# Half of the recurrence's input loads issued from ScalarE's queue instead of SyncE's

## The chip, the cores and the metric

The kernel runs on one core of a Trainium2 chip. The metric is the time of one execution on the device in microseconds (us). In what follows SP is SyncE, which here does nothing but issue transfers and wait; PE is TensorE, DVE is VectorE, ACT is ScalarE and POOL is GpSimd.

## What is computed

One step of a decoder layer for 2048 prompt tokens and 64 sample tokens (8 sequences of 8). A combined projection feeds two head groups, a chunked spatial gating and an S5 state-space layer; their outputs are merged by one projection, and a mixture of experts follows. The change lies in the S5 layer, whose core is a recurrence over positions:

```python
bu_re = jnp.einsum('blgh,gph->blgp', u, br)      # 32 groups of 16 channels, 64 complex states each
_, _, h_re, h_im = lax.associative_scan(ssm_combine, (a_re, a_im, bu_re, bu_im), axis=1)
y = (jnp.einsum('blgp,ghp->blgh', h_re, c_re) - jnp.einsum('blgp,ghp->blgh', h_im, c_im) + d_skip * u)
y = jax.nn.gelu(y.reshape(Bn, L, D_B))
```

## The kernel before

The program is a row of blocks with a barrier between them: the front (projections, tables), `s5` (the recurrence, 576 to 792 us of the span), `mixout`, routing, the experts and the final rows. In each block every engine has a hand-written list of instructions, ordered against the others by semaphores only.

**Layout in s5.** The prompt is cut into 128 chunks of 16 positions (Q = 16). `uT` holds the layer's input with a position within the chunk and a channel on the partitions: partition block m (16 partitions, the 16 channels of a group) holds position 7 - m of the first eight positions in `uT[:, 0]`, and position 15 - m in `uT[:, 1]`. The free axis runs over the 32 groups and over CH = 136 columns, 8 for the sample sequences and 128 for the chunks. The input lies in HBM (`s_d`, `ss_d`), written by the block before. One part of `uT`, eight groups, is loaded by `load_u(i)`: for two halves (kt) and eight blocks (m) one transfer of 64 KB for the prompt (L1243) and one of 4 KB for the samples (L1244), so 32 issues for a part and four parts in all.

**Tables.** `tab` has four slots and holds for a pair of groups what the recurrence multiplies by (768 KB, L1249); slot p % 4 may be loaded again when TensorE has finished the outputs of pair p - 4. `toep` (eight transfers of 256 KB, L1258) holds the part of the result that stays within eight positions.

**Work of a batch** b of two pairs. TensorE's `additions(b)` (L1319) makes the chunk's contribution to the state, from `uT` and `tab`; VectorE's `batch(b)` (L1407 to L1427) turns and scans it into the states `h`; TensorE's `outputs(2b)` and `outputs(2b+1)` (L1335, L1337, L1342) make the result, ScalarE puts it through gelu (L1383), and SP stores it with 24 transfers (L1270, L1273). TensorE's order is additions 0 and 1, then for each b: outputs 2b, outputs 2b+1, additions b+2. `additions(2j)` waits for part j of `uT`.

**SP's order**: tables 0 and 1, the two initial states, `load_u(0)`, `toep`, tables 2 and 3; then for each batch b: `load_u(b + 1)` while b < 3, tables 2b+4 and 2b+5, the 24 stores of batch b, which wait for its gelus.

**ScalarE's order**: it waits for TensorE's transpose of the initial states (`h0_mm`), copies them into `h` (L1373), makes the upper parts of two pieces of `w_glu` (`hi(0)`, `hi(1)`, L1369), and then does the gelus, with one more `hi` per batch. VectorE makes the matching lower parts (`low(0)`, `low(1)`, L1394) before `batch(0)`, and one `low` before each later batch. GpSimd loads the weights' pieces (L1297), from the third on each waiting for a `low`.

Of the kernel before, what the change touches and what calls it, by code (L numbers as in the profile page):

```python
# [41 lines left out]
GC = 16  # L42
# [4 lines left out]
CH = NCH + NSEQ  # L47
# [106 lines left out]
def build(nc, a, o):  # L154
    ctx = ExitStack()
    with ctx:
# [42 lines left out]
        with ExitStack() as mid:  # L199
            S.wout_hi = sb(mid, "wout_hi", [P, KD, D], F32R)  # L200
            S.wout_lo = sb(mid, "wout_lo", [P, KD, D], F32R)
            S.wglu_hi = sb(mid, "wglu_hi", [P, 4, DA], F32R)
            S.wglu_lo = sb(mid, "wglu_lo", [P, 4, DA], F32R)
            S.w_l = sem("weights_lo")
            s5(nc, S, a, o)
            spent.close()
            mixout(nc, S, a)
# [981 lines left out]
def s5(nc, S, a, o):  # L1189
    with ExitStack() as st:  # L1190
        sb, sem = S.sb, S.sem
        NB = 4
        uT = sb(st, "uT", [P, 2, G, CH])
        tab = sb(st, "tab", [P, NB, TABW])
        toep = sb(st, "toep", [P, G, P])
        h = sb(st, "h", [P, PAIRS, 2, CH + 1])
# [14 lines left out]
        u_ld = [sem(f"uT_loaded{i}") for i in range(4)]  # L1211
# [10 lines left out]
        N = NSEQ  # L1222

        def part(t_glu, t_out, n):
            return t_glu[:, 2 * n:2 * n + 2, :] if n < 2 else t_out[:, n - 2, :]

        def raw_part(n):
            return raw[:, n % 2, :].rearrange("p (k n) -> p k n", k=2) if n < 2 else raw[:, n % 2, :]

        w_glu, w_out = (t[0].rearrange("(k p) n -> p k n", p=P) for t in (a.w_glu, a.w_out))  # L1230

        with nc.Block() as block:
            @block.sync
            def _(sp):
                s_rows = S.s_d.rearrange("(g h) s c -> s h g c", h=GC)
                ss_rows = S.ss_d.rearrange("(g h) t q -> t h g q", h=GC)

                def load_u(i):
                    gs = slice(8 * i, 8 * i + 8)
                    for kt in range(2):  # L1240
                        for m in range(8):
                            rows = slice(m * GC, (m + 1) * GC)
                            sp.dma_start(uT[rows, kt, gs, N:CH], s_rows[8 * kt + 7 - m, :, gs, :]).then_inc(u_ld[i], 16)  # L1243
                            sp.dma_start(uT[rows, kt, gs, 0:N], ss_rows[7 - m, :, gs, :]).then_inc(u_ld[i], 16)  # L1244

                def load_tab(p):
                    if p >= NB:
                        sp.wait_ge(y_mm, 2 * (p - NB) + 2)
                    sp.dma_start(tab[:, p % NB, :], S.tab_d[p]).then_inc(tab_ld[p % NB], 16)  # L1249

                for p in range(2):
                    load_tab(p)
                for i, t in enumerate((a.state_ssm_re, a.state_ssm_im)):
                    sp.dma_start(h0_in[:, i, :], t[0].rearrange("q (a g) p -> (q a) (g p)", g=2)).then_inc(h0_ld, 16)
                load_u(0)
                for m in range(8):
                    s = 7 - m
                    sp.dma_start(toep[m * GC:(m + 1) * GC, :, :], S.kpad_d[:, :, P - s * GC:2 * P - s * GC]).then_inc(toep_ld, 16)  # L1258
                for p in range(2, 4):
                    load_tab(p)  # L1260

                def store_y(b):
                    g0 = 4 * b
                    sp.wait_ge(y_ok, 4 * b + 4)
                    for half in range(2):
                        for m in range(8):
                            dst = S.y_d.rearrange("(g o) s c -> s o g c", o=GC)[8 * half + m, :, g0:g0 + 4, :]
                            rows = slice(m * GC, (m + 1) * GC)
                            lo = N if half == 0 else CH
                            sp.dma_start(dst, ys[rows, b % 2, :, lo:lo + NCH]).then_inc(y_out[b % 2], 16)  # L1270
                    for m in range(8):
                        dst = S.ys_d.rearrange("(g o) t q -> t o g q", o=GC)[m, :, g0:g0 + 4, :]
                        sp.dma_start(dst, ys[m * GC:(m + 1) * GC, b % 2, :, 0:N]).then_inc(y_out[b % 2], 16)  # L1273

                for b in range(NBATCH):
                    if b < 3:
                        load_u(b + 1)
                    for p in (2 * b + 4, 2 * b + 5):
                        if p < PAIRS:
                            load_tab(p)  # L1280
                    store_y(b)
                sp.wait_ge(f_ok, 4)
                for i, (p, q) in enumerate(((o.ssm_re_prompt, o.ssm_re_sample), (o.ssm_im_prompt, o.ssm_im_sample))):
                    sp.dma_start(p[0, 0].rearrange("(a g) p -> a (g p)", g=2), po[:, i, :]).then_inc(f_out, 16)
                    sp.dma_start(q[0].rearrange("q (a g) p -> (q a) (g p)", g=2), fo[:, i, :]).then_inc(f_out, 16)
                sp.wait_ge(f_out, 64)
                for n in range(2):
                    sp.wait_ge(y_out[n], 16 * 24 * (NBATCH // 2))
# [76 lines left out]
            @block.scalar  # L1365
            def _(act):
                def hi(n):
                    act.wait_ge(raw_ld[n % 2], 16 * (n // 2) + 16)
                    act.activation(part(S.wglu_hi, S.wout_hi, n), raw_part(n), ACT.Copy).then_inc(w_h, 1)  # L1369

                act.wait_ge(h0_mm, 1)
                for i in range(2):
                    act.activation(h[:, :, i, 0:N], pY[:, 3, i * P:(i + 1) * P].rearrange("p (q a) -> p a q", q=NSEQ),  # L1373
                                   ACT.Copy).then_inc(h0_ok, 1)
                hi(0)
                hi(1)
                for p in range(PAIRS):
                    b = p // 2
                    for g in range(2):
                        act.wait_ge(y_mm, 2 * p + 2)  # L1380
                        if b >= 2:
                            act.wait_ge(y_out[b % 2], 16 * 24 * (b // 2))
                        act.activation(ys[:, b % 2, 2 * (p % 2) + g, 0:CH + NCH], pY[:, (2 * p + g) % 4, 0:CH + NCH],  # L1383
                                       ACT.Gelu_apprx_tanh).then_inc(y_ok, 1)
                    if p % 2 and p // 2 + 2 < 10:
                        hi(p // 2 + 2)
# [1174 lines left out]
```

## Time and profile before

| | |
|---|---|
| median of three runs | 1841.05 us (1839.16 to 1841.66) |
| the profiled execution | 1843.49 us, span 1841.4 us |
| TensorE busy, whole span | 1320.4 us, 72% |
| VectorE, ScalarE, GpSimd busy | 1012.7, 564.0, 387.5 us |
| mean granted TensorE clock | 0.839 of full speed |
| from 576 to 793 us: TensorE, VectorE, ScalarE busy | 92.2, 61.5, 20.6 us of 217 |

Busy time doesn't count the issuing of transfers, so SP's load is read from the timeline of its queue: start, duration of the issue, and the transfer's name. In a timeline the bracket at the end is the idle time before the instruction and who ended it. The DMA share is the mean busy share of the core's 16 DMA engines; it can exceed 1 where transfers of one engine overlap.

### The profile page before, as it was taken

The page shows a single profiled execution, that of the slowest core. Times are in us where ns is not written, and L with a number is a line of the kernel's source. Part 1 is how long each engine was busy: PE and PEld are TensorE (multiplying, and loading weights), DVE is VectorE, ACT ScalarE, POOL GpSimd, SP SyncE. Part 2 cuts the span into 40 slices and gives each one's busy share as a digit, 9 for nine tenths or more (in the row PEclk, how much of TensorE's full clock was granted, in tenths as well). Part 3 has the DMA queues.
Part 4 walks back from the last instruction along what each step waited for, and adds up shares of the span by engine and source line. Part 5 has one row for each costly group of instructions (what it writes and reads, how often), then busy time and mean ns, then how long its engine had stood idle before and what let it go on. Part 6 is the DMA issues. An engine that isn't in the chain of part 4 may idle for free. (4 is left out here: it accounts for less than half of the span.)

```text
span 1841.4 us, 25617 instructions
## 1 busy us (share of the span) xinstructions
PE 1320.4 (72%) x6602; PEld 1068.6 (58%) x6603; DVE 1012.7 (55%) x2397; ACT 564.0 (31%) x874; POOL 387.5 (21%) x392
## 2 busy tenths in 40 slices
PE   1466587999993435518888988379999999999300
PEld 0256465778872334417777876258777877777200
DVE  2355424776742233316666755858645477576398
ACT  2343320111111000113323221037645467566121
POOL 0020000222210000010010000035633337455321
PEclk9577688999997566759989998569999999999755
DMA  5966454753425945275544711269977679996597
GB/s 167 286 190 181 109 152 104 245 182 123 161 79 132 160 113 166 76 218 153 162 134 154 227 69 57 67 222 361 382 273 246 220 259 381 327 332 249 209 340 277
DMA packets 289969, 365.69 MB, mean 199 GB/s; under 512 B 125969, under 2 KB 229713, under 8 KB 286818
## 3 DMA queue, kind: packets, MB, share of 16 engines
q1 hardware_dynamic: 264770, 278.20, 48.3%
q0 software_dynamic: 25120, 86.53, 13.8%
q8 instruction: 38, 0.62, 0.1%
q14 instruction: 41, 0.34, 0.1%
HBM read 256.62 MB, written 108.04 MB: 198 GB/s over the span
## 5 line engine op out<-in xcount | busy, mean ns | idle before, releaser
L2222 POOL TENSOR_TENSOR down_lo<-expert_raw,down_hi (+1 forms) x64 | 153.1, 2415 | 198.2 <-ACT down_hi L2316 198.2
L2366 DVE TENSOR_TENSOR up_lo<-expert_raw,up_hi (+1 forms) x128 | 161.7, 1322 | 19.8 <-ACT up_hi L2311 17.3
L247 PE MATMUL ps_up<-up_hi,xT_hi 128*128 x400 | 161.5, 404 | 6.3 <-DVE up_lo L2366 2.9
L248 PE MATMUL ps_up<-up_lo,xT_hi 128*128 x400 | 156.7, 392 | 0.0
L249 PE MATMUL ps_up<-up_hi,xT_lo 128*128 x400 | 156.4, 391 | 0.0
L1610 PE MATMUL ps_out<-wout_hi,catT 128*128 128x512 f32 (+1 forms) x272 | 111.1, 408 | 24.5 <-DVE h L1764 22.1
L2311 ACT ACTIVATE up_hi<-expert_raw (+1 forms) x128 | 125.1, 1057 | 1.7 <-issue 0.5
L1611 PE MATMUL ps_out<-wout_lo,catT 128*128 128x512 f32 (+1 forms) x272 | 109.2, 402 | 0.0
L1612 PE MATMUL ps_out<-wout_hi,catT 128*128 128x512 f32 (+1 forms) x272 | 109.0, 401 | 0.0
L793 PE MATMUL ps_a<-hT,win_s 128*128 128x384 f32 (+2 forms) x160 | 69.9, 437 | 30.4 <-DVE sT L1089 30.3
L247 PEld LDWEIGHTS ps_up<-up_hi,xT_hi 128*128 128x128 f32 x400 | 75.5, 189 | 26.4 <-issue 11.7
L1319 PE MATMUL ps_state<-uT,tab 128*64 128x136 f32 (+1 forms) x256 | 28.6, 395 | 79.7 <-DMA tab<-s_tables 44.0
L249 PEld LDWEIGHTS ps_up<-up_hi,xT_lo 128*128 128x128 f32 x400 | 75.5, 189 | 16.2
L248 PEld LDWEIGHTS ps_up<-up_lo,xT_hi 128*128 128x128 f32 x400 | 75.6, 189 | 14.2
L2360 DVE TENSOR_TENSOR xT_lo<-ps_xT,xT_hi 128x512 fp32r<-128x512 f32 x102 | 65.7, 686 | 22.6 <-ACT xT_hi L2304 22.2
L249 PE MATMUL ps_y<-down_hi,hidT_lo 128*128 x196 | 77.6, 396 | 0.0
L247 PE MATMUL ps_y<-down_hi,hidT_hi 128*128 x196 | 77.5, 396 | 0.0
L248 PE MATMUL ps_y<-down_lo,hidT_hi 128*128 x196 | 77.5, 396 | 0.0
L2304 ACT ACTIVATE xT_hi<-ps_xT 128x512 fp32r<-128x512 f32 x102 | 55.4, 598 | 69.3 <-PE ps_xT L2252 68.9
L1576 POOL DMA_DIRECT2D expert_rows<-blank x31 | 26.8, 984 | 232.7 <-DVE x L1767 228.8
L1610 PEld LDWEIGHTS ps_out<-wout_hi,catT 128*128 128x128 f32 (+1 forms) x272 | 52.3, 192 | 37.9 <-DVE h L1764 22.6
L1394 DVE TENSOR_TENSOR wout_lo<-weights_raw,wout_hi 128x1024 fp32r<-128x1024 f32 x8 | 9.8, 1226 | 116.8 <-ACT wout_hi L1369 116.8
(392 smaller groups left out, 3180.0 us busy)
## 6 DMA issues: line engine op xcount, KB each, us to landing
expert_raw<-in_w SPq DMA_DIRECT2D x96, 1024.0 KB, 7.8
expert_rows<-yo SPq DMA_DIRECT2D x49, 512.0 KB
x<-in_x_prompt SPq DMA_DIRECT2D x32, 512.0 KB, 5.2
stage<-in_w_ada SPq DMA_DIRECT2D x16, 1024.0 KB
expert_rows<-blank POOLq DMA_DIRECT2D x31, 512.0 KB, 5.6
tab<-s_tables SPq DMA_DIRECT2D x16, 768.0 KB, 4.6
h_turned<-hT SPq DMA_DIRECT2D x48, 192.0 KB, 2.1
hT<-h_turned SPq DMA_DIRECT2D x48, 192.0 KB, 2.9
```

The lines of the kernel that those rows point to most:

```text
L247: pe.matmul(out, left(0, k), right(0, k), start=k == 0, stop=False)
L248: pe.matmul(out, left(0, k), right(1, k), start=False, stop=False)
L249: last = pe.matmul(out, left(1, k), right(0, k), start=False, stop=k == n - 1)
L793: pe.matmul(out[:, j, 0:w], hi[:, k, cols], hT[:, 0, k, 0:w], start=k == 0, stop=False)
L1610: pe.matmul(out, cat[:, 0, k, ts], S.wout_hi[:, k, cols], start=k == 0, stop=False)
L1611: pe.matmul(out, cat[:, 0, k, ts], S.wout_lo[:, k, cols], start=False, stop=False)
L1612: last = pe.matmul(out, cat[:, 1, k, ts], S.wout_hi[:, k, cols], start=False, stop=k == KD - 1)
L2222: pool.tensor_tensor(down_piece(down_lo, run, m), raw_piece(run, 2, m, 1), down_piece(down_hi, run, m).bitcast(F32), ALU.subtract).then_in ...
L2304: act.activation(xT_hi[:, par, 4 * h:4 * h + 4, :], pX[:, h, :].rearrange("p (k t) -> p k t", k=4), ACT.Copy).then_inc(x_a, 1)
L2311: act.activation(up_piece(up_hi, run, m), raw_piece(run, m // 2, m % 2, KD // 2), ACT.Copy).then_inc(up_h, 1)
L2360: dve.tensor_tensor(xT_lo[:, par, ks, :], pX[:, h, :].rearrange("p (k t) -> p k t", k=4), xT_hi[:, par, ks, :].bitcast(F32), ALU.subtract) ...
L2366: dve.tensor_tensor(up_piece(up_lo, run, m), raw_piece(run, m // 2, m % 2, KD // 2), up_piece(up_hi, run, m).bitcast(F32), ALU.subtract).t ...
```

## The change

The second half of every part (kt = 1, positions 8 to 15 of a chunk) is issued by ScalarE. SP keeps the first half. ScalarE issues its 4 x 16 transfers at the head of the block, ahead of its first wait; SP's order is otherwise the same. The semaphores and the counts that TensorE waits for (32 transfers a part) stay.

```diff
+        s_rows = S.s_d.rearrange("(g h) s c -> s h g c", h=GC)
+        ss_rows = S.ss_d.rearrange("(g h) t q -> t h g q", h=GC)
+
+        def load_half(eng, i, kt):
+            gs = slice(8 * i, 8 * i + 8)
+            for m in range(8):
+                rows = slice(m * GC, (m + 1) * GC)
+                eng.dma_start(uT[rows, kt, gs, N:CH], s_rows[8 * kt + 7 - m, :, gs, :]).then_inc(u_ld[i], 16)
+                eng.dma_start(uT[rows, kt, gs, 0:N], ss_rows[7 - m, :, gs, :]).then_inc(u_ld[i], 16)
+
         with nc.Block() as block:
             @block.sync
             def _(sp):
-                s_rows = S.s_d.rearrange("(g h) s c -> s h g c", h=GC)
-                ss_rows = S.ss_d.rearrange("(g h) t q -> t h g q", h=GC)
-
                 def load_u(i):
-                    gs = slice(8 * i, 8 * i + 8)
-                    for kt in range(2):
-                        for m in range(8):
-                            rows = slice(m * GC, (m + 1) * GC)
-                            sp.dma_start(uT[rows, kt, gs, N:CH], s_rows[8 * kt + 7 - m, :, gs, :]).then_inc(u_ld[i], 16)
-                            sp.dma_start(uT[rows, kt, gs, 0:N], ss_rows[7 - m, :, gs, :]).then_inc(u_ld[i], 16)
+                    load_half(sp, i, 0)
...
+                for i in range(4):
+                    load_half(act, i, 1)
                 act.wait_ge(h0_mm, 1)
```

## Rows read from the trace of the kernel before

**Rows 1.** Waits, 576 to 795 us: who waited for what, total us, times, longest.
```profile
PE ps_state L1319 <- DMA tab<-s_tables: 44.0, 10, 16.1
```

**Rows 2.** Timeline of SP's queue, 560 to 800 us: start, us, issue.
```profile
576.84 0.82 SPq L1249 DMA_DIRECT2D tab<-s_tables  x2
...
578.88 0.65 SPq L1243 DMA_DIRECT2D uT<-s_in  x1
...
594.88 0.43 SPq L1244 DMA_DIRECT2D uT<-s_in_sample  x1
595.36 11.26 SPq L1258 DMA_DIRECT2D toep<-toeplitz_rows  x8
606.65 2.93 SPq L1249 DMA_DIRECT2D tab<-s_tables  x2
609.63 0.99 SPq L1243 DMA_DIRECT2D uT<-s_in  x1
...
631.74 2.81 SPq L1249 DMA_DIRECT2D tab<-s_tables  x2
634.92 7.53 SPq L1270 DMA_DIRECT2D s_out<-ys  x16
642.49 4.83 SPq L1273 DMA_DIRECT2D s_out_sample<-ys  x8
647.36 0.42 SPq L1243 DMA_DIRECT2D uT<-s_in  x1
...
662.39 0.43 SPq L1244 DMA_DIRECT2D uT<-s_in_sample  x1
662.87 0.91 SPq L1249 DMA_DIRECT2D tab<-s_tables  x2
...
677.22 0.43 SPq L1243 DMA_DIRECT2D uT<-s_in  x1
...
692.56 0.90 SPq L1249 DMA_DIRECT2D tab<-s_tables  x2
...
705.08 2.97 SPq L1249 DMA_DIRECT2D tab<-s_tables  x2
```

**Rows 3.** Timeline of TensorE, 560 to 800 us; in brackets the wait before it.
```profile
601.31 3.79 PE L1319 MATMUL ps_state<-uT,tab 128*64 128x136 f32 x32 [12.46 <-DMA uT<-s_in_sample]
621.22 2.03 PE L1319 MATMUL ps_state<-uT,tab 128*64 128x136 f32 x16 [16.12 <-DMA tab<-s_tables]
624.20 2.03 PE L1319 MATMUL ps_state<-uT,tab 128*64 128x136 f32 x16 [0.95 <-DMA tab<-s_tables]
626.16 1.28 PE L1335 MATMUL ps_s<-uT,toep 128*128 128x136 f32 x4
...
667.32 2.03 PE L1319 MATMUL ps_state<-uT,tab 128*64 128x136 f32 x16 [16.05 <-DMA tab<-s_tables]
...
697.08 4.15 PE L1319 MATMUL ps_state<-uT,tab 128*64 128x136 f32 x32 [19.55 <-issue]
```

**Rows 4.** Busy time by stretch; the last two columns are DMA share and GB/s.
```profile
590.00:594.00 4.00, 0.00 (x0) 0.00 (x0) 2.36 (x2) 1.22 (x2) 1.12 (x2) 0.50 0.67 120
598.00:616.00 18.00, 3.79 (x32) 3.42 (x32) 5.90 (x18) 0.00 (x0) 0.00 (x0) 0.50 1.27 114
618.00:621.00 3.00, 0.00 (x0) 0.00 (x0) 0.00 (x0) 0.00 (x0) 0.00 (x0) 0.50 1.00 384
647.40:662.80 15.40, 3.87 (x38) 3.08 (x36) 7.03 (x19) 2.29 (x5) 0.53 (x1) 0.72 0.42 102
677.20:692.50 15.30, 0.33 (x6) 0.14 (x4) 7.03 (x19) 1.62 (x3) 0.53 (x1) 0.64 0.48 103
```

**Rows 5.** Timeline of VectorE, 560 to 680 us.
```profile
590.31 2.36 DVE L1394 TENSOR_TENSOR wglu_lo<-weights_raw,wglu_hi 128x1024 fp32r<-128x1024 f32 x2 [18.14 <-ACT wglu_hi L1369]
605.24 0.42 DVE L1407 TENSOR_TENSOR turned<-ps_state,tab 128x256 f32<-128x256 f32 x1 [12.57 <-PE ps_state L1319]
...
610.96 0.42 DVE L1427 TENSOR_TENSOR h<-turned 128x256 f32<-128x256 f32 x1
...
659.90 0.42 DVE L1427 TENSOR_TENSOR h<-turned 128x256 f32<-128x256 f32 x1
```

**Rows 6.** The page's costliest groups: issues on GpSimd, count, busy, mean ns.
```profile
L1576 POOL DMA_DIRECT2D expert_rows<-blank x31 | 26.8, 984 | 232.7 <-DVE x L1767 228.8
```

**Rows 7.** Timeline of ScalarE, 560 to 640 us.
```profile
588.88 0.46 ACT L1373 ACTIVATE h<-ps_s 128x128 f32<-128x128 f32 x2 [24.23 <-PE ps_s L1303]
589.22 2.00 ACT L1369 ACTIVATE wglu_hi<-weights_raw 128x1024 fp32r<-128x1024 f32 x2
```

## The prediction

> **What bounds the stage now.** I read the waits first. In the recurrence stage TensorE mostly waits, and the transfers it waits for are the tables: ten waits, 44.0 us [rows 1]. A table is only 768 KB, so the question is why it arrives late, and that is answered by the timeline of SP's queue [rows 2]. Between 631.74 and 708 us SP issues back to back. There is no wait in it worth a microsecond: two tables, the 24 stores of batch 0 (634.92 to 647.32), the 32 loads of uT part 2 (647.36 to 662.83), two tables (662.87), 24 stores, the 32 loads of part 3 (677.22 to 692.5), two tables (692.56), 24 stores, tables (705.08). The table issued at 662.87 is what TensorE starts on at 667.32, after 16.05 us of waiting, and the one issued at 692.56 is behind the start at 697.08 [rows 3]. So in these two periods the rate at which SP can issue is the bound, not the transfers: while part 2 was issued the DMA engines had a busy share of 0.42 and while part 3 was, 0.48 [rows 4]. From 705.08 on there are no input loads left, SP waits for TensorE and the period is the compute chain's.
>
> The head of the stage is different. Part 0 is issued from 578.88 to 595.3, toep until 606.6, tables 2 and 3 until 609.6 [rows 2]. TensorE starts the first additions at 601.31, then waits 16.12 us for table 2 (621.22) and a little for table 3 (624.20), and the first outputs start at 626.16 [rows 3]; call that moment T. Here the DMA engines are full: from 598 to 616 their share is 1.27 and yet they move only 114 GB/s, while at 618 to 621, when the tables go, a share of 1.00 moves 384 GB/s [rows 4]. The head is bound by slow transfers as much as by issue. The eight toep transfers (256 KB each, into 16 partitions each) alone are 2.1 MB, 18 us at 114 GB/s.
>
> **The change, part by part.** *Removed from SP:* half of each part, 16 of 32 issues, four times. Part 2 cost 647.36 to 662.87, 15.51 us, half is 7.76. Part 3 cost 677.22 to 692.56, 15.34 us, half is 7.67. Nothing waits in between, so tables 6 and 7 come 7.8 us earlier and tables 8 and 9 15.4 us earlier, both counted from T. What is late next? VectorE's h of batch 2, at 660.3 us [rows 5], would let outputs start at T + 34.2. TensorE would start additions(3) at 667.32 - 7.76, that is T + 33.4, and needs about 4.1 us for them, so those outputs start at T + 37.5. SP stays the bound with 3 us to spare, and both halves are gained in full. From table 10 (705.08) on, SP waits for TensorE as before and nothing more is gained. Part 1 ended at 631.7, about when TensorE had finished the first outputs, which release table 4. That half is mostly hidden: I give it 0.6 us. **Term one: 7.76 + 7.67 + 0.6 = 16.0 us, counted from T.**
>
> *Added to ScalarE:* 64 issues ahead of its wait for h0_mm. The trace has no issue on ScalarE. The nearest row from below is SP's own: 32 issues in 578.88 to 595.36, 0.51 us each, and in the undisturbed part 3 0.48 us. The nearest from above is GpSimd's issue, 984 ns [rows 6], made by another way of issuing. I take SP's: the same kind of instruction, 64 x 0.48 = 31 us, from about 576.8 to 607.5. Behind them on ScalarE stand the two h0 copies (588.88 now), the splits of w_glu (589.22) [rows 7]; behind those VectorE's low(0), low(1) (590.31), then its batch 0 (605.24) [rows 5], and GpSimd's next two loads of w_out. From h0 copy to the end of low takes 588.88 to 592.67, 3.8 us, and a batch takes 605.24 to 611.38, 6.1 us. So h of batch 0 comes at 607.5 + 3.8 + 6.1 = 617.4 us, against 611.4 now. TensorE needs it at T, 626.16 now: the cover is the wait for tables 2 and 3, and it is 8.8 us thick after the change if T stays. The later splits of ScalarE and its gelus start after 631 and aren't touched. If an issue costs 0.98 us, h comes at 576.8 + 63 + 9.9 = 649.7 and T is 23.5 us later.
>
> *Moved in the head:* SP reaches toep 16 issues earlier, 16 x 0.48 = 7.7 us, and tables 2 and 3 behind it. If ScalarE's loads cost these transfers nothing, T is 626.2 - 7.7 = 618.5, just after h at 617.4. But ScalarE puts the second halves of parts 1 to 3 into the DMA engines in just this stretch: 24 pairs of 64 KB + 4 KB, 1.67 MB that used to move after 610 us. Like toep they go to 16 partitions each. If they take their turn with toep at the 114 GB/s of [rows 4], they cost 14.6 us and T is 618.5 + 14.6 = 633.1, 6.9 us later than now. If they overlap wholly, the 7.7 us are kept. For some overlap speak the DMA share of 0.67 at 590 to 594, which is room, and that w_out's 1 MB leaves the stretch for later; against it, the share of 1.27 for the 18 us after. I take the middle, a cost of 6.5 us: T = 625.0. **Term two: +1.2 us, between +7.7 and -6.9.**
>
> The Trainium skill bears on this term (SBUF — State Buffer, "Door 1: The DMA port swizzle"): 16 neighbouring partitions reach four of sixteen ports, some 109 GB/s; the trace agrees, 114 GB/s at 598 to 616. [...] Another page speaks against the change (DMA: Bandwidth & Descriptors, "Issuing engines are not separate DMA queues"): issuing from a second engine saves only the sequencer's time, "usually small relative to the DMA itself". By it the sum would be near 0; that is the third rival.
>
> **The sum.** 16.0 + 1.2 = 17.2 us, against the profiled execution's own 1843.49 us (span 1841.4): 1826.3. The median of the runs is 1841.05, 2.4 lower, and the forecast is for that: 1841.05 - 17.2 = 1823.9 us. Nothing else changes: the stages are separate blocks, and the mixing stage starts its loads once this block has ended (792 us), so a gain in the stage is a gain of the kernel.
>
> **Rivals.**
> 1. *The head overlaps better than I think* (the DMA engines take both queues side by side): T = 618.5, gain 16.0 + 7.7 = 23.7, 1817.4 us. For it: the room at 590 to 594. Against: the share of 1.27.
> 2. *The head is serial*: every byte that ScalarE brings forward delays tables 2 and 3; T = 633.1, gain 16.0 - 6.9 = 9.1, 1832.0 us. For it: 114 GB/s at full share. Against: the overlap that different row blocks may have.
> 3. *Issue was not the limit*: parts 2 and 3 take as long with half the issues because the transfers do, and the time stays, 1841. Against it: shares of 0.42 and 0.48, and an issue every 0.48 us with no wait.
> 4. *ScalarE's issue is slow* and h of batch 0 becomes what T waits for. With an issue at 0.98 us T is 649.7, which costs 23.5 and leaves 16.0 - 23.5 = -7.5: 1848.6 us, slower. It decides from T = 642.2 on, that is h0 copies at 632.3, 0.87 us an issue. For it: SP itself fell to (631.74 - 609.63)/32 = 0.69 us when its queue met a full DMA, and ScalarE will issue into just that stretch [rows 2]. At 0.69 us T would be 576.8 + 44.2 + 9.9 = 630.9 us, still a gain of 11.
>
> **Chances.** Forecast (gain 13 to 20) 0.50; rival 1 0.17; rival 2, with rival 4's mild form, 0.23; rival 3 0.05; rival 4 in full 0.05. The two outer gains are inside the range, so it goes from 1817 to 1833 us. A change of 0.2% (3.7 us) is what a measurement of this kernel can tell. Faster: 0.50 + 0.17 + 0.23 + a little of rivals 3 and 4, 0.91; same 0.05; slower 0.04.
>
> **What the profile after would show.** Right: uT loads on ScalarE's queue, 64 from about 577 to 607 us; 16 issues of some 7.7 us per part on SP; tables 6 and 7 issued about T + 29 (now T + 36.7), tables 8 and 9 T + 51 (now T + 66.4); unchanged periods of some 17.5 us from table 10 on; the stage's end 17 us earlier. Term two is read from T alone: what TensorE's first L1335 waited for, a table (DMA-bound head) or h (ScalarE late). Wrong would be: periods 2 and 3 shortened by less than 7 us each, which kills term one; T beyond 633; or the gain given back after 792 us.

## The result, and the profile after

The changed kernel is slower: median 1875.47 us of four runs (1867.05 to 1879.24) against 1841.36 us (1839.16 to 1850.72), ratio 1.0169 with a 95% interval of 1.0118 to 1.0220. Forecast were 1823.9 us and a range of 1817 to 1833. The profiled execution, 1867.05 us, is the fastest of the four; its span is 1865.2 us, that of the profiled execution before is 1841.4.

The loss doesn't lie where the change was made. SP's timeline after the change, to be held against [rows 2]:

```profile
573.37 0.81 SPq L1251 DMA_DIRECT2D tab<-s_tables  x2
...
585.62 17.61 SPq L1260 DMA_DIRECT2D toep<-toeplitz_rows  x8
603.26 3.65 SPq L1251 DMA_DIRECT2D tab<-s_tables  x2
...
636.84 3.40 SPq L1251 DMA_DIRECT2D tab<-s_tables  x2
...
652.79 0.43 SPq L1239 DMA_DIRECT2D uT<-s_in  x1
...
660.37 0.90 SPq L1251 DMA_DIRECT2D tab<-s_tables  x2
...
681.90 0.90 SPq L1251 DMA_DIRECT2D tab<-s_tables  x2
...
695.17 2.13 SPq L1251 DMA_DIRECT2D tab<-s_tables  x2
...
782.18 17.49 SPq L1527 DMA_DIRECT2D yf<-s_out  x4
```

The last line is the next block's first load. The recurrence's block took 782.18 - 573.37 = 208.8 us; before it was 792.77 - 576.84 = 215.9. So at 782 us the changed kernel is 10.6 us ahead, 7.1 of them from this block (the rest is the front, which differs by that much from run to run). From there to the end it takes 1865.2 - 782.2 = 1083.0 us where 1048.6 were needed, with no line of that code changed. That is 34.4 us lost.

TensorE's timeline, for [rows 3]:

```profile
596.29 3.79 PE L1321 MATMUL ps_state<-uT,tab 128*64 128x136 f32 x32 [10.21 <-DMA uT<-s_in_sample]
620.20 2.03 PE L1321 MATMUL ps_state<-uT,tab 128*64 128x136 f32 x16 [20.12 <-DMA tab<-s_tables]
623.63 2.03 PE L1321 MATMUL ps_state<-uT,tab 128*64 128x136 f32 x16 [1.41 <-DMA tab<-s_tables]
631.38 1.25 PE L1337 MATMUL ps_s<-uT,toep 128*128 128x136 f32 x4 [5.72 <-DVE h L1431]
...
664.72 2.03 PE L1321 MATMUL ps_state<-uT,tab 128*64 128x136 f32 x16 [7.52 <-DMA tab<-s_tables]
...
686.34 4.17 PE L1321 MATMUL ps_state<-uT,tab 128*64 128x136 f32 x32 [6.50 <-issue]
```

T, the start of the first outputs, is 631.38 - 573.37 = 58.0 us after the block's first issue, before it was 626.16 - 576.84 = 49.3. From T to the block's end it is 150.8 us in place of 166.6. So the periods gained 15.8 us, and the head lost 8.7 of them. What TensorE waited for last at T was VectorE's h, 5.72 us. Behind that stand ScalarE and VectorE (first the last of ScalarE's 64 issues, then the lines of [rows 7] and [rows 5]):

```profile
620.89 0.45 ACTq L1240 DMA_DIRECT2D uT<-s_in_sample  x1
621.39 0.46 ACT L1377 ACTIVATE h<-ps_s 128x128 f32<-128x128 f32 x2 [60.20 <-issue]
621.72 2.00 ACT L1371 ACTIVATE wglu_hi<-weights_raw 128x1024 fp32r<-128x1024 f32 x2
```
```profile
622.81 2.36 DVE L1398 TENSOR_TENSOR wglu_lo<-weights_raw,wglu_hi 128x1024 fp32r<-128x1024 f32 x2 [54.12 <-ACT wglu_hi L1371]
625.09 0.42 DVE L1411 TENSOR_TENSOR turned<-ps_state,tab 128x256 f32<-128x256 f32 x1
...
630.82 0.42 DVE L1431 TENSOR_TENSOR h<-turned 128x256 f32<-128x256 f32 x1
```

ScalarE issued from 573.37 to 621.34, 0.75 us an issue on average: some 0.5 us where its queue met no obstacle, but one issue of 5.57 us and one of 2.35 while toep and the tables went.

Of the 34.4 us lost later, SP's timeline shows where the most went. At the end of the experts' block, first before and then after the change (`expert_rows<-yo` are its stores, `gate_sample` is the final block's first load):

```profile
1689.34 29.62 SPq L2197 DMA_DIRECT2D expert_rows<-yo  x4
1726.03 2.71 SPq L2440 DMA_DIRECT2D gate_sample<-ada_rows  x8
```
```profile
1686.36 28.95 SPq L2201 DMA_DIRECT2D expert_rows<-yo  x4
1748.80 2.72 SPq L2444 DMA_DIRECT2D gate_sample<-ada_rows  x8
```

Between SP's last store and the next block lay 1726.03 - 1718.96 = 7.1 us, and now 1748.80 - 1715.31 = 33.5. In this time SP goes through the passes of the experts' loop whose steps are all skipped: the loop is made for the largest number of expert blocks, 64, and guards each step by a branch; 49 blocks were stored here, so that the last three of its 15 passes do nothing. That is 26.4 us more for skipping. Another 7.1 us went in the passes that do work (from the experts' first weight load to the last store 539.4 us in place of 532.3), and 1 in the final block. The page's list of queues has the trace of it; the columns are packets, MB and share:

```profile
q14 instruction: 41, 0.34, 0.1%
```
```profile
q10 hardware_dynamic: 9216, 2.23, 1.2%
q14 instruction: 111, 0.91, 0.1%
```

Before, 41 packets of some 8 KB brought instructions in on that queue; after, 111. (q10 is ScalarE's new queue.) The engines fetched code 70 times more. Asked stretch by stretch, the trace says where: up to the experts' first weight load q14 had 28 packets before and 29 after. In the experts' block before, all 11 came in its first 153 us and none in the 379 us from 1340 us to the last store, nor in the pause behind it; after the change 50 came from 1330 us to the last store and 17 more in the pause. So the fetching goes on as long as the experts' loop does, in code that nobody touched.

### The profile page after: what moved, and what is told of

Read it like the earlier page. It is cut to its first block and busy times, and to the rows that moved or that the text cites. A ratio compares the mean times of both kernels' runs of the same rounds, so it can differ in the third digit from the quotient of the medians.

```text
span 1865.2 us, 25617 instructions
## 1 busy us (share of the span) xinstructions
PE 1320.3 (71%) x6602; PEld 1068.4 (57%) x6603; DVE 1013.6 (54%) x2397; ACT 563.3 (30%) x874; POOL 388.1 (21%) x392
## 5 line engine op out<-in xcount | busy, mean ns | idle before, releaser
L2226 POOL TENSOR_TENSOR down_lo<-expert_raw,down_hi (+1 forms) x64 | 152.8, 2409 | 205.1 <-ACT down_hi L2320 205.1
L247 PEld LDWEIGHTS ps_up<-up_hi,xT_hi 128*128 128x128 f32 x400 | 75.6, 189 | 26.5 <-issue 11.7
L2320 ACT ACTIVATE down_hi<-expert_raw (+1 forms) x64 | 64.2, 1052 | 34.0 <-issue 18.6
```

Source lines behind the costliest of these rows:

```text
L247: pe.matmul(out, left(0, k), right(0, k), start=k == 0, stop=False)
L2226: pool.tensor_tensor(down_piece(down_lo, run, m), raw_piece(run, 2, m, 1), down_piece(down_hi, run, m).bitcast(F32), ALU.subtract).then_in ...
L2320: act.activation(down_piece(down_hi, run, m), raw_piece(run, 2, m, 1), ACT.Copy).then_inc(down_h, 1)
```

## The experiments

**Which list moved the loop?** The change takes 64 instructions from SP's list and adds 64 to ScalarE's, and both lists have the experts' loop behind that point. Four kernels separate them. The filling is an increment of a semaphore that nobody reads, put where the engine waits anyway:

```diff
 # route, SP's list
+                for _ in range(64):          # 192 in the fourth
+                    sp.sem_inc(pad_s, 1)
                 sp.wait_ge(tables_ok, 1)
 # experts, ScalarE's list
+                for _ in range(192):         # 64 in the third
+                    act.sem_inc(pad_s, 1)
                 evac_x(0, 0)
```

> The changed kernel, with 64 one-line instructions (increments of a semaphore that nobody reads) put into SP's list in the routing block, where SP waits anyway. That gives SP's list its old length ahead of the experts' loop. In the traces the recurrence block is 7.1 us shorter after the change (215.9 to 208.8 us) and all that follows it 34.4 us longer (1048.6 to 1083.0). Theory 1, SP's expert loop has moved to a place in its instruction memory where it is fetched again on every pass: the later blocks are back at about 1049 us, the instruction packets of the page's queue q14 fall from 111 to about 41, and the time is about 1841 - 7 = 1834 us. Theory 2, it is ScalarE's list, 64 longer: no change, 1870 us and some 110 packets. Theory 3, placement has nothing to do with it (a second hardware queue in use, or chance): no change either.

> The changed kernel, with 192 increments of an unread semaphore at the head of ScalarE's list in the experts' block, where ScalarE idles 57 us. Its list had grown by 64, so its loop is now 256 instructions further on than before the change, the same place for any block size that divides 256. Theory 2 (ScalarE's placement): about 1834 us and some 41 instruction packets on q14. Theory 1 (SP's placement) and theory 3 (no placement): as after the change, 1870 us, some 110 packets.

> The kernel before, with 64 such increments at the head of ScalarE's list in the experts' block: ScalarE's loop stands where the change put it, and nothing else is changed. Theory 2: about 1841 + 30 = 1871 us and some 110 instruction packets on q14. Theories 1 and 3: 1841 us, some 41 packets.

> The kernel before, with 192 such increments in SP's list in the routing block. The change took 64 instructions out of that list; 192 more are the same shift for any block size that divides 256. Theory 1: about 1841 + 30 = 1871 us and some 110 instruction packets on q14. Theories 2 and 3: 1841 us, some 41 packets.

| | SP's loop | ScalarE's loop | packets on q14 | ratio to before (95%) | block end to span end |
|---|---|---|---|---|---|
| before | 1132 | 790 | 41 | 1 | 1048.6 us |
| after | 1068 | 854 | 111 | 1.0169 (1.0118 to 1.0220) | 1083.0 |
| after, SP + 64 | 1132 | 854 | 41 | 0.9983 (0.9963 to 1.0003) | 1056.5 |
| after, ScalarE + 192 | 1068 | 1046 | 113 | 1.0227 (1.0193 to 1.0260) | 1092.0 |
| before, ScalarE + 64 | 1132 | 854 | 41 | 0.9998 (0.9980 to 1.0015) | 1051.3 |
| before, SP + 192 | 1324 | 790 | 113 | 1.0203 (1.0167 to 1.0238) | 1086.5 |

The two columns of loops count the instructions of that engine's built list ahead of its experts' loop. The loss comes and goes with SP's column: 1132 is fast, 1068 and 1324 (256 further on) are slow. SP's filling itself costs nothing; from its last store ahead of the experts' block to the first expert weights it is 43.8 us, start to start, in the kernel before, after the change and in both fillings. ScalarE's 192 were not free: its first work of the experts' block begins 36.3 us behind the first weight load in place of 30.6, and that is 5.7 of the 9.0 us by which this profile's later blocks exceed those after the change. The kernel before, with the recurrence as it was and only SP's loop shifted, is 2.0% slower, without a second queue in use; the changed kernel with SP's loop put back has lost the loss (1840.49 us, where 1834 was expected). Its timeline has the 7.1 us at the end again (1726.27 - 1719.19):

```profile
1689.90 29.29 SPq L2204 DMA_DIRECT2D expert_rows<-yo  x4
1726.27 2.72 SPq L2447 DMA_DIRECT2D gate_sample<-ada_rows  x8
```

SP's loop is 286 instructions long in the built list (one fewer than an expectation below says). The Trainium skill (Runtime: NRT & Kernel Launch, "Instruction fetch mechanics") says that an engine other than TensorE keeps 512 instructions in two blocks of 256, and that "Branching breaks sequential prefetch": a target outside of the two costs a fetch before execution goes on. The packets that go on through the loop, some 4.7 more for each of its 15 passes, and the pause at the end agree with that as a kind of event. As an estimate from the page's figures, 286 instructions lie over three blocks for 29 of 256 starting places and over two for the others. No run here looked at which places those are, so that the loop lay over three blocks is not shown.

**The place alone, mended differently.** The changed kernel with SP's loop told where to start:

```diff
-            with eng.Fori(1, NBLK // AHEAD) as j:
+            head = {eng.engine: 0} if eng.engine == mybir.EngineType.SP else None
+            with nc.Fori(1, NBLK // AHEAD, engines=bass.OrderedEngineSet([eng.engine]), head_slot=head) as j:
```

> The changed kernel as it is, except that SP's expert loop is told to start at slot 0 of an instruction block. If the place of that loop is the whole of the loss behind the recurrence, the packets on q14 are near 41 in place of 111, the pause on SP between the last store of the experts and the final block's first load is about 7 us in place of 33.5, and the time is that of the changed kernel with SP's list at its old length, about 1841 us.

Measured: 42 packets, the pause 7.2 us, median 1843.64 us, ratio 0.9993 (0.9979 to 1.0007). The place accounts for the whole loss, as far as these runs can tell. The run also says what the edit is worth without it: 0.07%, or 0.17% by the other mend. Both intervals reach 1, so no gain is shown. The recurrence's block is 209.4 us in this profile, 6.5 below the before's 215.9, so 0.35% could be expected. The rest is in the later blocks: 1054.1 us in place of 1048.6, of which the experts' block has 4.6 (543.96 in place of 539.33). The just-in-time kernel with the same mend (below) shows 544.1 there too, and no other kernel without the loss shows more than 542.3, so I take slot 0 for a place that is somewhat worse than the old one; why is open. In the first experiment it is the mixing and routing blocks that took 3.2 us more (397.1 in place of 393.9). Three kernels below have the same 397 us there, the others 393.6 to 394.0, and that code is the same in all but the filling; that is open too.

**What cost the head its 8.7 us?** Four kernels, all with SP's list filled up to its old length.

> The changed kernel with SP's list at its old length (the 64 increments of the first experiment), and ScalarE's loads of parts 1 to 3 behind its copies of h0 and its first two splits; only part 0's half stands ahead of them. The stage's block takes 209.3 us with SP's length mended and all loads ahead. Theory A: the head lost mainly because ScalarE came late, TensorE's first outputs waited 5.7 us for h after table 3 had come; then they start with the tables, some 52.4 us after the block's first issue in place of 58, and the block takes about 203.5 us. Theory B: the head lost because the transfers that ScalarE brings forward delay the tables, which this order doesn't change: the tables still come at 47 and 50.5 us. A and B can both hold, the first for 5.7 us, the second for 3. If neither holds, the block stays at 209 us.

```diff
-                for i in range(4):
-                    load_half(act, i, 1)
+                load_half(act, 0, 1)
                 act.wait_ge(h0_mm, 1)
...
                 hi(1)
+                for i in range(1, 4):
+                    load_half(act, i, 1)
```

The next two keep `load_half(act, 0, 1)` ahead of the wait; in the second of them it is all that ScalarE issues.

> As the experiment before it, but ScalarE issues the halves just in time: part 1's behind its first two splits, part 2's behind the gelus of batch 0, part 3's behind those of batch 1. Theory B: with 16 of 24 pairs gone from the head, tables 2 and 3 come at 37 to 42 us after the block's first issue, the first outputs start at 42 to 46 in place of 49.3 before the change, and the block takes 193 to 197 us. If the tables don't depend on that traffic, they stay at 47 and 50.5 and the block at about 203 us. With the later blocks as before the change the time is about 1844 - 20 = 1824 us.

```diff
                 hi(1)
+                load_half(act, 1, 1)
                 for p in range(PAIRS):
...
                         hi(p // 2 + 2)
+                    if p in (1, 3):
+                        load_half(act, p // 2 + 2, 1)
```

> One part of the change alone: only the second half of part 0 is ScalarE's. SP reaches toep some 6 to 7 us earlier than before the change. The prediction's step: tables 2 and 3 come 7.7 us earlier, at 37 and 40 us after the block's first issue, and the block takes 208 us. Theory C, the head is bound by its transfers and not by SP's issue: the tables stay at 44 and 47 us within 2 us, only the first additions come a little earlier, and the block takes about 215 us as before.

```diff
                     load_half(sp, i, 0)
+                    if i:
+                        load_half(sp, i, 1)
```

> Term one alone: parts 0 and 1 are loaded wholly by SP, as before the change, and only the second halves of parts 2 and 3 are ScalarE's, issued behind the gelus of batches 0 and 1. SP's list is filled up to its old length with 32 increments. The head should be as before (first outputs 49.3 us after the block's first issue), and from there to the block's end 166.6 - 15.4 = 151.2 us; the block takes about 200.5 us, the kernel about 1829 us. If the two periods were not bound by SP's issue, the block stays at 216.

Here SP's list has both halves of parts 0 and 1, and ScalarE's has the two lines under `if p in (1, 3)`. The table's columns are in us after the block's first issue, each the difference of two starts in the timelines; "table 2" and "table 3" are the starts of the additions that waited for them:

| | table 2 | table 3 | first outputs (T) | T to block's end | block |
|---|---|---|---|---|---|
| before | 44.4 | 47.4 | 49.3 | 166.6 | 215.9 |
| after | 46.8 | 50.3 | 58.0 | 150.8 | 208.8 |
| after, SP + 64 | 47.8 | 50.7 | 58.8 | 150.5 | 209.3 |
| parts 1 to 3 behind the splits | 49.8 | 52.4 | 53.9 | 148.8 | 202.7 |
| just in time | 47.5 | 50.2 | 52.2 | 150.4 | 202.6 |
| part 0's half alone | 45.0 | 48.3 | 50.2 | 166.2 | 216.4 |
| parts 2 and 3 alone | 44.5 | 47.5 | 49.4 | 155.7 | 205.1 |

Each row is one profile. Kernels with the same code in this block show how far such a row can be trusted: 215.9, 212.7 and 216.2 us for the kernel before and its two fillings, 208.8 to 209.6 for the changed one in four kernels, 202.6 and 205.8 for the two just-in-time kernels. Table 2 came at 43.6 to 44.8 us in the first three and at 46.2 to 47.8 in the next four. Blocks that differ by less than some 3 us, and tables that differ by less than 1.5, are not told apart here.

Behind the splits, TensorE starts the first outputs as soon as table 3's additions are done and waits for h no more; the end of the head in that kernel:

```profile
626.01 2.03 PE L1321 MATMUL ps_state<-uT,tab 128*64 128x136 f32 x16 [23.84 <-DMA tab<-s_tables]
628.62 1.59 PE L1321 MATMUL ps_state<-uT,tab 128*64 128x136 f32 x16 [0.58 <-DMA tab<-s_tables]
630.14 0.73 PE L1337 MATMUL ps_s<-uT,toep 128*128 128x136 f32 x4
```

So theory A held, for 4 to 5 us. Theory B's forecast, tables at 37 to 42 us, missed: with 16 of the 24 pairs gone from the head, the just-in-time kernel has its tables at 47.5 and 50.2, no earlier than after the change, and its block is no shorter than that of the kernel with all of them there. And part 0's half alone, which was to bring the tables 7.7 us forward, brings nothing:

```profile
601.44 3.79 PE L1323 MATMUL ps_state<-uT,tab 128*64 128x136 f32 x32 [9.60 <-DMA uT<-s_in_sample]
624.27 2.03 PE L1323 MATMUL ps_state<-uT,tab 128*64 128x136 f32 x16 [19.04 <-DMA tab<-s_tables]
627.53 2.03 PE L1323 MATMUL ps_state<-uT,tab 128*64 128x136 f32 x16 [1.23 <-DMA tab<-s_tables]
629.49 1.28 PE L1339 MATMUL ps_s<-uT,toep 128*128 128x136 f32 x4
```

The block began at 579.28, so table 2 is at 45.0. SP did reach toep early, and then stood in it:

```profile
590.98 19.38 SPq L1262 DMA_DIRECT2D toep<-toeplitz_rows  x8
```

That is 11.7 us after the block's first issue in place of 18.5, but the eight issues took 19.4 us in place of 11.3 [rows 2], and ended at the same place within 1.3 us. Some of the 19.4 us may be due to `w_out`'s two loads, 1.05 MB: GpSimd issues them 15 to 17 us after the block's first issue in either kernel, which was ahead of toep and is now behind its start. The kernel after the change, where these loads come 51 us after the first issue, says the same of toep: reached at 12.3 us, done at 29.9, before it was 29.8. Theory C, the head is bound by its transfers, is the one that holds. The whole kernels came out at a ratio of 0.9957 (0.9941 to 0.9974) with the loads behind the splits, 0.9954 (0.9938 to 0.9969) just in time, 1.0003 (0.9991 to 1.0015) for part 0 alone, 0.9928 (0.9906 to 0.9951) for parts 2 and 3 alone. Of the last, the expected 151.2 us from T to the end were 155.7, a gain of 10.9 us where 15.4 were expected: SP's first stores began 10.0 us after T in place of 8.8, and the later tables landed later after their issue (6.4 us in place of 4.5 for table 6).

> The just-in-time order without the 64 increments; in their place SP's expert loop is told to start at slot 0 of an instruction block, so that the code ahead of it can't shift it. If the later blocks' loss comes from where SP's loop (287 instructions) lies over the instruction blocks, the packets on q14 stay near 41 and the time is that of the just-in-time kernel with increments, about 1824 us. If it comes from the length of SP's list as such, the packets are at about 110 and the time is 30 us above it.

Measured: 42 packets, 1840.93 us, ratio 0.9967 (0.9952 to 0.9982). The length of SP's list is not the cause, the loop's place is. The ratio is 0.13% above that of the kernel with the filling, and the intervals overlap; the slot may be the reason again.

**Part 1 wholly on SP.**

> Candidate for the best: ScalarE issues the second halves of part 0 (ahead of its first wait) and of parts 2 and 3 (behind the gelus of batches 0 and 1); part 1 is wholly SP's again, since its loads are the ones that met toep and the tables. SP's list is filled up to its old length. With part 1's half out of the head, tables 2 and 3 should come at or before 44.4 and 47.4 us after the block's first issue, where they came before the change, in place of 47.5 and 50.2 with part 1's half in the head. Then the block takes 196 to 203 us and the kernel about 1830 us; if the tables stay at 47.5, part 1's half was not what delayed them, and the block takes 203 to 206.

```diff
                     load_half(sp, i, 0)
+                    if i == 1:
+                        load_half(sp, i, 1)
```

Measured: tables at 45.4 and 48.9, T at 50.8, block 202.4 us, median 1832.5 us, ratio 0.9936 (0.9919 to 0.9953). The tables were expected at or before 44.4 and 47.4 and missed that. They stand some 2 us ahead of the just-in-time kernel's at table 2 and not ahead of the kernel before, as theory C has it; the block is no shorter than the just-in-time kernel's 202.6. The ratio's interval meets those of the just-in-time kernel and of parts 2 and 3 alone (0.9928), so the best of the three is not told; all are faster than the kernel before by 0.5 to 0.7%.

## Why the prediction was wrong, point by point

**SP's issue bounds periods 2 and 3, and half of it is gained in full (term one, 16.0 us).** Right in this profile: from T to the end 15.8 us were gained; start of additions(3) at T + 33.3 (forecast 33.4), of additions(4) at T + 55.0 in place of 70.9. Part 0's half alone, with SP's loads of parts 1 to 3 whole, keeps 166.2 of the 166.6. "In full" is more than all runs bear: with the head as it was and parts 2 and 3 alone on ScalarE it was 10.9 of 15.4 us, and where T came late, as after the change, some of the gain from T may be owed to that. Rival 3, that issue was not the limit, is out for the periods. In the head it was what happened.

**The head (term two, +1.2 us between +7.7 and -6.9).** It was -8.7, outside of both bounds. Two steps of it failed. "SP reaches toep 16 issues earlier, ... and tables 2 and 3 behind it": reaching toep early moved no table, since toep's transfers were the slow part and SP's time in them grew from 11.3 to 17.6 us, by what was saved ahead of them (6.3). The gain of 7.7 us that both bounds began from didn't exist; table 3 came 2.9 us later than before. The second: "an issue every 0.48 us" on ScalarE. It was 0.75, with the two long issues while the DMA share was 1.23; h came 57.9 us after the block's first issue where the forecast has 40.6, and T waited for it 5.7 us. Table 3's delay and this wait make up the 8.7 us. Rival 4 had this mechanism, in its mild form, but priced at 0.69 us an issue. The overlap itself, taken at a middle of 6.5 us, was priced somewhat too high: against part 0's half alone, 24 pairs delayed table 2 by 1.8 to 4.8 us, and 598 to 616 us moved 143 GB/s in place of 114 [rows 4]:

```profile
598.00:616.00 18.00, 2.08 (x20) 1.68 (x16) 0.00 (x0) 0.00 (x0) 0.00 (x0) 0.50 1.28 143
```

So the two queues together moved a quarter more than SP's alone, at the same share of 1.27 to 1.28. Why they overlap in part isn't shown: no run varied which row blocks are filled at a time.

**"Nothing else changes ... a gain in the stage is a gain of the kernel."** This is the step that decided. It was argued from barriers and data alone and left out that a list of instructions is also code at a place. Taking 64 instructions from SP's list shifted a loop of 286 that begins some hundreds of instructions later, and code was fetched all through that loop where none had been: 34.4 us in the profile, 2.0% by the kernel before with SP's loop shifted alone. Without it the forecast of 17.2 us would still have been too high: with the place mended the edit came out at 0.07 and 0.17%, neither clear of 1, and the block itself at 7.1 us.

**What the profile after was to show**: the 64 issues end at 621 and not at 607, tables 6 and 7 are issued at T + 29.0 (forecast 29), tables 8 and 9 at T + 50.5 (forecast 51), the later periods, from 706 us on, are 17.3 to 17.8 us. "The gain given back after 792 us" was among the signs of a wrong prediction, but no rival had a mechanism for it.

## What to carry to other kernels

When a change adds or removes many instructions, look for loops behind them in the same engine's list before any time is forecast: compare the page's instruction packets before and after, and pin the loop's place or fill the list up, or a good edit is read as a bad one (and the reverse). Whether a stretch in which a queue issues back to back is bound by the issue could be read here from the DMA engines' share: at a share of 0.42 to 0.48 half the issues gave 7.8 us a period back (10.9 of 15.4 us in the least good case), at 1.27 they gave nothing. Loads that are handed to a second engine go behind that engine's first needed work; how far behind made no difference here (0.9957 and 0.9954).

## What the runs showed of the hardware

The place of a loop in an engine's instruction list alone is worth 2.0% of this kernel (1.0203, interval 1.0167 to 1.0238, for 192 instructions that do nothing), with 113 instruction packets in place of 41; the loop's skipped passes took SP 33.5 us with the fetches and 7.1 without. A ScalarE issue took 0.48 us on average for the 16 of part 2 in the kernel with parts 2 and 3 alone, and up to 5.57 us in the head after the change, where the DMA share was 1.23. Two queues whose transfers mostly write blocks of 16 partitions moved 143 GB/s together, and SP's alone 114.
